# The order of two steps in the state-space scan: both halves of the x_dt transposes in one place, the product of the decay across chunks behind the segment sums

## The chip, the cores and the metric

The kernel runs on one core of one Trainium2 chip. The metric is the device time of one execution in microseconds (us). The changed kernel is timed against the one before; the time given is the median of several executions.

## The reference

One layer of a hybrid decoder: a Mamba-2 state-space branch (SSD) and a sparse attention branch work on the same normalised input of 256 tokens and 1024 channels, and are merged by gates. What matters here is the SSD branch, cut to its core:

```python
xdt = (xh * dt[..., None])                      # 32 heads of 64, 2 chunks of 128 tokens
a_cs = jnp.cumsum(adt, axis=2)                  # adt = dt * a
seg = a_cs[:, :, :, None] - a_cs[:, :, None, :]
decay = jnp.exp(jnp.where(causal, seg, -jnp.inf))
cb = jnp.einsum('bclgn,bcsgn->bclsg', c_, b_)
y_diag = jnp.einsum('bclsg,bclsgh,bcsghp->bclghp', cb, decay, xdt)
...
y_off = jnp.einsum('bclgn,bcghpn,bclgh->bclghp', c_, prev, jnp.exp(a_cs))
y = (y_diag + y_off) + xh * d_skip
y = rmsnorm_by_group(y * silu(z))               # 4 groups of 512 channels
```

The 32 heads form 4 groups of 8 heads. With only two chunks, the state that chunk 0 hands to chunk 1 needs no recurrence: its part of y is a product with a third decay matrix, "across" the two chunks.

## The kernel before

All weights come as 133 units of 128x1024 float32 (512 KB each) through seven buffers `w_raw`. Almost every unit (a split unit) is made into a high part `w_hi` by ACT (L924) and a low part `w_lo`, of which DVE subtracts the first six or seven eighths (L1185) and POOL the rest (L1527). PE then needs 24 matmuls of 256 columns for the unit (L696 to L698: high by high, low by high, high by low), into one of three banks `gemm0` to `gemm2`. ACT and DVE read the tile out.

What each engine does, and in what order, is one hand-written table, `schedule()`. `put(u, ...)` hangs steps behind unit u. PE and POOL work through it in the order STEPS: unit u, then its steps. ACT and DVE work through LATE_STEPS: the steps of unit u stand one unit later, behind what they do for unit u+1. No engine leaves its own order; semaphores alone join them.

Units 13 to 44 are the projections x and z: four x tiles and four z tiles for each group. The scan of group g is hung at b = 20 + 8g and what follows, so b is unit 20, 28, 36 and 44. The steps are, with q a half group of four heads (a quad, two for each group):

- xt (g, c): PE transposes the four x tiles of chunk c into a small bank (L743); DVE multiplies them by dt into `x_dt` (L1382) and sets the bank free.
- seg q: PE forms the segment sums of both chunks in the two score banks (L757, L758); ACT takes the exponential (L1082, `decay`); DVE multiplies chunk 0 by C·B (L1389, `cb_decay`), POOL chunk 1 (L1588).
- ea q: PE forms the sums across the chunks in a small bank (L764); ACT takes the exponential (L1088, `decay_across`); POOL multiplies by C·B (L1599, `cb_decay_across`) and then makes the rows `seg_moving` for the next quad (L1539, two instructions).
- y q: PE multiplies (L784 with `cb_decay`, L787 with `cb_decay_across`) into the bank `y_or_o`; DVE adds the skip (L1395) and multiplies by the z gate (L1400).
- ysq, ysum, ssq, yn: the norm of the group before. ACT squares (L1093), POOL adds up (L1593, L1594), PE sums over the partitions in a small bank (L794), ACT takes the root (L1098, with a table load before and after it), DVE takes the reciprocal (L1404) and normalises (L1409, L1413).

There are two small banks, used in turn by all steps that need one. Before a step writes its bank, PE waits until the step two before it has been read out:

```python
def begin_small(key):
    n = T_IDX[key]
    if n >= 2:
        pe.wait_ge(t_free[n % 2], n // 2)
    return TB[n % 2]
```

The order of use within a group is xt (g, 0), xt (g, 1), ea 2g, ssq g-1, ea 2g+1. So ea 2g waits for the DVE instruction L1382 of xt (g, 0), and ssq g-1 for that of xt (g, 1). The step ssq g-1 also waits for POOL's two sums; y q waits for L1389, L1588 and L1599 of its quad. Below, a scan step's number is that of its quad, 0 to 7.

Of the kernel before, what the change touches and what calls it, by code (L numbers as in the profile page):

```python
# [77 lines left out]
def schedule():  # L78

    after = {}

    def put(u, *steps):
        after.setdefault(u, []).extend(steps)

    put(len(PAIRS) - 2, ("ada2", 0))
    put(6, ("dtT", 0))
    put(7, ("dtA", 0), ("dtE", 0))
    put(8, ("dtB", 0), ("dtL", 0))
    put(10, ("dtC", 0))
    put(13, ("acs", 0))
    for kind in range(3):  # L100
        put(15 + kind, ("cb", kind))
    ssq_after = 12
    for g in range(SSM_GROUPS):
        b = 20 + 8 * g
        put(b, ("xt", (g, 0)))
        put(b + 1, ("xt", (g, 1)), ("seg", 2 * g))
        put(b + 2, ("ea", 2 * g))
        put(b + 4, ("y", 2 * g), ("seg", 2 * g + 1))
        put(b + 5, ("ea", 2 * g + 1))
        put(b + 7, ("y", 2 * g + 1))  # L110
        put(b + 8, ("ysq", g))
        put(b + 10, ("ysum", g))
        put(b + ssq_after, ("ssq", g))
        for j in range(TPG + 2):
            for ahead, name in ((2, "ynlo"), (1, "ynhi"), (0, "yn")):
                if 0 <= j - ahead < TPG:
                    put(b + ssq_after + 2 + j, (name, TPG * g + j - ahead))
    for g in range(KV_GROUPS):
        put(18 + 8 * g, ("blk0", g))
        put(19 + 8 * g, ("blk1", g))  # L120
    put(47, ("clear", 0))
    at = UNITS.index
    put(at(("w1k", 0, 3)) + 2, ("hidT", 0))
    put(at(("w1v", 0, 3)) + 2, ("hidT", 1))
    put(at(("w1v", 0, 3)) + 1, ("kcp", 0))
    put(at(("w1v", 0, 3)) + 4, ("vcp", 0))
    put(at(("vs", 1, 0)) + 2, ("vt", 0))
    put(at(("w1v", 0, 3)) + 3, ("zero", 0))
    tiles = [u for u, unit in enumerate(UNITS) if unit[0] != "ag"]
    q7 = tiles.index(at(("q", 7, 0)))  # L130

    def after_tile(n, *steps):
        put(tiles[n], *steps)

    after_tile(q7 + 1, ("cs", 0), ("cs", 1))
    after_tile(q7 + 2, ("cs2", 0))
    after_tile(q7 + 3, ("vt", 1))
    after_tile(q7 + 5, ("ct", 0), ("ct", 1))
    t0 = q7 - 2
    after_tile(t0 - 3, ("kpos", 0))  # L140
    for h in range(ATT_HEADS):
        after_tile(t0 - 2 + 2 * h, ("q2", h))
    for h in range(ATT_HEADS):
        after_tile(t0 + 2 * h, ("sc", h))
        after_tile(t0 + 1 + 2 * h, ("ex", h))
        after_tile(t0 + 2 + 2 * h, ("ps", h))
        after_tile(t0 + 4 + 2 * h, ("pt", h))
    last_h = tiles.index(at(("mg", 15, 0)))
    for p in range(ATT_HEADS // 2):
        after_tile(t0 + 8 + 4 * p + (p == 0), ("pv", p))  # L150
        after_tile(max(last_h + 3, t0 + 8 + 4 * p), ("osp", p))
    put(at(("nsa", 4, 0)), ("agB", 0))
    put(at(("nsa", 6, 0)), ("agB", 1))
    steps = []
    for u in range(len(UNITS)):
        steps.append(("gemm", u))
        steps += after.get(u, [])
    steps += [("flush", 0)]

    late = []  # L160
    for u in range(len(UNITS)):
        late += [("gemm", u)] + after.get(u - 1, [])
    late += [("flush", 0)] + after.get(len(UNITS) - 1, [])
    return steps, late


STEPS, LATE_STEPS = schedule()
SPLIT_IDX, NATIVE_IDX, TILE_IDX = {}, {}, {}
for _u, (_kind, _j, _part) in enumerate(UNITS):
# [1582 lines left out]
```

## Time and profile before

| | us |
|---|---|
| median of 3 runs | 475.51 |
| lowest and highest | 475.44, 476.58 |
| the profiled execution | 475.58 |
| its span in the trace | 473.8 |
| PE busy | 439.2 (93%) |
| DVE busy | 353.0 (75%) |
| ACT busy | 264.7 (56%) |
| POOL busy | 231.1 (49%) |

The profiled execution lies within 0.1 us of the median. The span is 1.8 us shorter than its time; what lies around it has no instructions. In the views below a matmul's duration runs from its start to its modelled end, so starts are read against starts. "Idle before" is time in which an engine had nothing running, with what released it.

### The profile page before, as it was taken

The numbers are of one execution on the slowest core, as the hardware profiler recorded it, in microseconds if no ns is written. First come the engines' busy times: TensorE is split into PE (matmuls) and PEld (weight loads), VectorE is DVE, ScalarE is ACT, GpSimd is POOL, SyncE is SP. The second block draws the span as 40 slices with busy tenths as digits, with TensorE's granted clock in tenths as the row PEclk, the third lists the DMA queues.
The fourth block names the chain that finished last, engine by engine and source line by source line (L and its number), as shares of the span: only waits on it lengthen the run. The fifth ranks groups of instructions, "written<-read, shape, count | busy, mean of one in ns | idle before, by whom it ended". The sixth has DMA issues, their size and how long they took to land.

```text
span 473.8 us, 9880 instructions
## 1 busy us (share of the span) xinstructions
PE 439.2 (93%) x3640; PEld 402.2 (85%) x3640; DVE 353.0 (75%) x617; ACT 264.7 (56%) x518; POOL 231.1 (49%) x236
## 2 busy tenths in 40 slices
PE   2689989999999996999889999999999999999995
PEld 2287989999999986987789999889898999999874
DVE  0375789999999999968684876768696766547733
ACT  3245785755566646644697844656566464534441
POOL 0154662368697557683365542244445362445340
PEclk9779999999999998999999998999999999999999
DMA  8998544564424532527609840625747433556102
GB/s 291 420 413 343 180 135 133 192 205 139 151 74 134 177 117 70 178 84 260 224 6 385 291 170 0 222 96 218 258 144 255 147 126 122 162 193 246 46 0 89
DMA packets 22391, 84.04 MB, mean 177 GB/s; under 512 B 2492, under 2 KB 2882, under 8 KB 21186
## 3 DMA queue, kind: packets, MB, share of 16 engines
q1 hardware_dynamic: 22344, 83.42, 49.7%
q8 instruction: 29, 0.48, 0.4%
q14 instruction: 18, 0.15, 0.1%
HBM read 82.36 MB, written 1.05 MB: 176 GB/s over the span
## 4 chain that ended last, share of the span: by engine, by line
PE 70%; DVE 9%; issue 7%; ACT 5%; POOL 4%; DMA 3%; SPq 1%; DVEq 0%; POOLq 0%; ACTq 0%
PE gemm L696 15%; PE gemm L698 15%; PE gemm L697 15%; DMA w_ada_shift_scale<-in_w_ada 3%; PE y_or_o L902 2%; DVE w_lo L1185 2%; ACT w_hi L924 2%; PE y_or_o L784 1%; DVE conv_acc L1232 1%; ACT probs L1143 1%; PE score L866 1%; POOL w_lo L1527 1%; PE small L577 1%; PE gemm L655 1%; PE score L868 1%
## 5 line engine op out<-in xcount | busy, mean ns | idle before, releaser
L1527 POOL TENSOR_TENSOR w_lo<-w_raw,w_hi 128x256 fp32r<-128x256 f32 (+1 forms) x117 | 132.2, 1135 | 175.6 <-ACT w_hi L924 140.9
L696 PE MATMUL gemm<-h_hi,w_hi 128*128 128x256 f32 x600 | 173.1, 289 | 2.7 <-DVE conv_acc L1232 2.0
L697 PE MATMUL gemm<-h_lo,w_hi 128*128 128x256 f32 x600 | 168.5, 281 | 0.0
L698 PE MATMUL gemm<-h_hi,w_lo 128*128 128x256 f32 x600 | 168.4, 281 | 0.0
L1185 DVE TENSOR_TENSOR w_lo<-w_raw,w_hi 128x768 fp32r<-128x768 f32 (+1 forms) x117 | 132.0, 1129 | 43.6 <-ACT w_hi L924 42.9
L924 ACT CAST w_hi<-w_raw 128x1024 fp32r<-128x1024 f32 x117 | 122.1, 1046 | 52.4 <-PE gemm L698 29.4
L696 PEld LDWEIGHTS gemm<-h_hi,w_hi 128*128 128x128 f32 x600 | 114.7, 191 | 5.4 <-issue 2.5
L697 PEld LDWEIGHTS gemm<-h_lo,w_hi 128*128 128x128 f32 x600 | 114.2, 190 | 0.5
L698 PEld LDWEIGHTS gemm<-h_hi,w_lo 128*128 128x128 f32 x600 | 114.5, 191 | 0.0
L696 PE MATMUL gemm<-ynorm_hi,w_hi 128*128 128x256 f32 x128 | 36.4, 284 | 0.0
L698 PE MATMUL gemm<-ynorm_hi,w_lo 128*128 128x256 f32 x128 | 35.6, 278 | 0.0
L697 PE MATMUL gemm<-ynorm_lo,w_hi 128*128 128x256 f32 x128 | 35.6, 278 | 0.0
L1232 DVE SCALAR_TENSOR_TENSOR conv_acc<-gemm,conv_half,conv_acc 128x255 f32<-128x255 f32 (+2 forms) x66 | 31.6, 479 | 2.8 <-ACT conv_acc L957 1.2
L1143 ACT ACTIVATE probs<-score,softmax_small 128x128 f32<-128x128 f32 (+1 forms) x64 | 26.0, 422 | 1.5 <-DVE softmax_small L1448 1.5
L957 ACT ACTIVATE conv_acc<-gemm,conv_half 128x256 f32<-128x256 f32 x22 | 12.4, 564 | 25.1 <-DVE x_conv_T L1194 15.4
L1588 POOL TENSOR_TENSOR cb_decay<-decay,cb_T 128x512 f32<-128x512 f32 x8 | 12.1, 1511 | 27.0 <-ACT decay L1082 19.3
L696 PEld LDWEIGHTS gemm<-ynorm_hi,w_hi 128*128 128x128 f32 x128 | 24.1, 188 | 0.7 <-issue 0.7
L1539 POOL TENSOR_TENSOR seg_moving<-acs_rows,consts 128x512 fp32r<-128x512 f32 x16 | 20.6, 1309 | 8.2 <-DVE acs_cols L1374 8.2
L698 PEld LDWEIGHTS gemm<-ynorm_hi,w_lo 128*128 128x128 f32 x128 | 24.2, 189 | 0.0
L697 PEld LDWEIGHTS gemm<-ynorm_lo,w_hi 128*128 128x128 f32 x128 | 24.0, 188 | 0.0
L1150 ACT COPY probs_T<-small 128x512 f32<-128x512 f32 x16 | 9.5, 593 | 19.8 <-PE y_or_o L902 19.8
L931 ACT ACTIVATE tanh_tmp<-gemm 128x256 f32<-128x256 f32 x24 | 9.2, 385 | 19.5 <-PE gemm L698 17.4
(253 smaller groups left out, 897.3 us busy)
## 6 DMA issues: line engine op xcount, KB each, us to landing
w_raw<-in_wpack SPq DMA_DIRECT2D x133, 512.0 KB, 4.3
w_ada_shift_scale<-in_w_ada SPq DMA_DIRECT2D x8, 1024.0 KB, 15.7
x_T<-in_xT SPq DMA_DIRECT2D x2, 512.0 KB, 5.9
x_residual<-in_x_tok SPq DMA_DIRECT2D x1, 1024.0 KB, 4.8
out_tok_dram<-out_tok SPq DMA_DIRECT2D x4, 256.0 KB, 2.1
ada_gate_products<-in_gate_bias SPq DMA_DIRECT2D x1, 512.0 KB, 4.8
g_post_rows<-in_g_post_rows SPq DMA_DIRECT2D x1, 512.0 KB, 5.7
consts<-in_consts SPq DMA_DIRECT2D x1, 272.0 KB, 22.7
```

Source lines behind the costliest of these rows:

```text
L696: nc.tensor.matmul(bank[:, 0:SEQ], w_hi, hi[:, k0 + k, :], start=first, stop=False)
L697: nc.tensor.matmul(bank[:, 0:SEQ], w_hi, lo[:, k0 + k, :], start=False, stop=False)
L698: last = nc.tensor.matmul(bank[:, 0:SEQ], w_lo, hi[:, k0 + k, :], start=False, stop=end)
L924: nc.scalar.copy(WH[:, n % HI_SLOTS, :], RAW[:, u % RAW_SLOTS, :]).then_inc(hi_ready, 1)
L957: nc.scalar.activation(ACC[:, ci % 2, :], bank, ACT.Identity, bias=CW[:, 96 + col:97 + col], scale=CW[:, 4 * col + 3:4 * col + 4]).then_in ...
L1143: last = nc.scalar.activation(E[:, k, b, P * qt:P * qt + nk], SB[qt][:, nk * b:nk * b + nk], ACT.Exp, bias=SM[:, k, 0, c:c + 1], accum_out ...
L1150: nc.scalar.copy(PT[:, i % 2, :, 0:SEQ], bank[:, :].rearrange("p (b q) -> p b q", b=2)).then_inc(release, 1)
L1185: nc.vector.tensor_tensor(WL[:, n % LO_SLOTS, 0:c], RAW[:, u % RAW_SLOTS, 0:c], WH[:, n % HI_SLOTS, 0:c], ALU.subtract).then_inc(lo_ready, 1)
L1232: ins = nc.vector.scalar_tensor_tensor(ACC[:, ci % 2, s:SEQ], bank[:, 0:SEQ - s], CW[:, 4 * col + tap:4 * col + tap + 1], ACC[:, ci % 2, s ...
L1527: nc.gpsimd.tensor_tensor(WL[:, n % LO_SLOTS, c:1024], RAW[:, u % RAW_SLOTS, c:1024], WH[:, n % HI_SLOTS, c:1024], ALU.subtract).then_inc( ...
L1539: nc.gpsimd.tensor_tensor(MV[:, c, :, :], TP[:, c, :].unsqueeze(1).to_broadcast([P, 4, P]), oh, ALU.mult).then_inc(mv_done, 1)
L1588: nc.gpsimd.tensor_tensor(MM[:, 1, :, :], EX[:, 1, :, :], CB[:, 1, i // 2, :].unsqueeze(1).to_broadcast([P, 4, P]), ALU.mult).then_inc(mm_ ...
```

## The change

In the part of `schedule()` for the scan, xt (g, 1) moves from unit b+1 to unit b, ea 2g from b+2 to b+1, and ea 2g+1 from b+5 to b+4. Since the table drives all engines, the transposes, DVE's products by dt, ACT's exponential, POOL's product and POOL's next rows all move with their step.

```diff
     for g in range(SSM_GROUPS):
         b = 20 + 8 * g
-        put(b, ("xt", (g, 0)))
-        put(b + 1, ("xt", (g, 1)), ("seg", 2 * g))
-        put(b + 2, ("ea", 2 * g))
-        put(b + 4, ("y", 2 * g), ("seg", 2 * g + 1))
-        put(b + 5, ("ea", 2 * g + 1))
+        put(b, ("xt", (g, 0)), ("xt", (g, 1)))
+        put(b + 1, ("seg", 2 * g), ("ea", 2 * g))
+        put(b + 4, ("y", 2 * g), ("seg", 2 * g + 1), ("ea", 2 * g + 1))
         put(b + 7, ("y", 2 * g + 1))
         put(b + 8, ("ysq", g))
         put(b + 10, ("ysum", g))
```

No instruction is added or removed, and the order in which the small banks are used stays as it was. The changed file has two lines less, so in its rows every line number from there on is smaller by 2.

On PE at seg 6 (group 3, unit b+1 = 45), before:

```order
L698 MATMUL gemm2<-h_hi_52,w_lo_56 128x256
L743 MATMUL small0<-consts_60,x_conv_T_89 128x128 x4
L757 MATMUL score0<-seg_moving_95,acs_cols_72 128x512
L758 MATMUL score0<-mask_sl_bf16_62,ident_bf16_61 128x512
L757 MATMUL score1<-seg_moving_95,acs_cols_72 128x512
L758 MATMUL score1<-mask_sl_bf16_62,ident_bf16_61 128x512
L696 MATMUL gemm0<-h_hi_52,w_hi_55 128x256
```

and in the change:

```order
L696 MATMUL gemm2<-h_hi_52,w_lo_56 128x256
L755 MATMUL score0<-seg_moving_95,acs_cols_72 128x512
L756 MATMUL score0<-mask_sl_bf16_62,ident_bf16_61 128x512
L755 MATMUL score1<-seg_moving_95,acs_cols_72 128x512
L756 MATMUL score1<-mask_sl_bf16_62,ident_bf16_61 128x512
L762 MATMUL small1<-seg_moving_95,acs_cols_72 128x512
L694 MATMUL gemm0<-h_hi_52,w_hi_55 128x256
```

The transposes of chunk 1 into `small0` have gone ahead of unit 45, and ea 6 into `small1` stands ahead of unit 46, where it used to stand behind it.

On DVE at the same place, where `x_dt` is made, before:

```order
L1194 SCALAR_TENSOR_TENSOR z_gate_then_y_75<-tanh_tmp_108,gemm1 128x256
L1185 TENSOR_TENSOR w_lo_56<-w_raw_54,w_hi_55 128x768
L1413 TENSOR_TENSOR ynorm_lo_77<-y_tmp_101,ynorm_hi_76 128x256
L1409 SCALAR_TENSOR_TENSOR y_tmp_101<-z_gate_then_y_75,params_59,rstd_y_102 128x256
L1382 TENSOR_TENSOR x_dt_92<-small1,dt_68 128x512
L1194 SCALAR_TENSOR_TENSOR z_att_then_o_78<-tanh_tmp_108,gemm2 128x256
```

and in the change:

```order
L1192 SCALAR_TENSOR_TENSOR z_gate_then_y_75<-tanh_tmp_108,gemm1 128x256
L1183 TENSOR_TENSOR w_lo_56<-w_raw_54,w_hi_55 128x768
L1411 TENSOR_TENSOR ynorm_lo_77<-y_tmp_101,ynorm_hi_76 128x256
L1407 SCALAR_TENSOR_TENSOR y_tmp_101<-z_gate_then_y_75,params_59,rstd_y_102 128x256
L1380 TENSOR_TENSOR x_dt_92<-small1,dt_68 128x512
L1380 TENSOR_TENSOR x_dt_92<-small0,dt_68 128x512
L1192 SCALAR_TENSOR_TENSOR z_att_then_o_78<-tanh_tmp_108,gemm2 128x256
```

The instruction that frees `small1` for ea 6 keeps its place in DVE's order; the one that frees `small0` follows it at once.

On POOL around quad 6, before:

```order
L1588 TENSOR_TENSOR cb_decay_97<-decay_96,cb_T_93 128x512
L1527 TENSOR_TENSOR w_lo_56<-w_raw_54,w_hi_55 128x256
L1593 TENSOR_TENSOR y_sq_100<-y_sq_100 128x512
L1594 TENSOR_TENSOR y_sq_100<-y_sq_100 128x256
L1599 TENSOR_TENSOR cb_decay_across_99<-decay_across_98,cb_T_93 128x512
L1539 TENSOR_TENSOR seg_moving_95<-acs_rows_71,consts_60 128x512 x2
```

and in the change:

```order
L1586 TENSOR_TENSOR cb_decay_97<-decay_96,cb_T_93 128x512
L1597 TENSOR_TENSOR cb_decay_across_99<-decay_across_98,cb_T_93 128x512
L1537 TENSOR_TENSOR seg_moving_95<-acs_rows_71,consts_60 128x512 x2
L1525 TENSOR_TENSOR w_lo_56<-w_raw_54,w_hi_55 128x256
L1591 TENSOR_TENSOR y_sq_100<-y_sq_100 128x512
L1592 TENSOR_TENSOR y_sq_100<-y_sq_100 128x256
```

The across product and the next rows come first now, and the two sums for the norm of the group before stand behind them. Quads 2 and 4 have the same pattern.

## Rows read from the trace of the kernel before

**Rows 1.** Waits of PE alone, 100 to 215 us: us, times, longest.
```profile
PE y_or_o L784 <- POOL cb_decay_across L1599: 5.7, 3, 4.2
```

**Rows 2.** Timeline of PE, y 5 and after: start, us, [idle before <-releaser].
```profile
180.38 0.28 PE L698 MATMUL gemm<-h_hi,w_lo 128*128 128x256 f32 x1
184.82 0.66 PE L784 MATMUL y_or_o<-cb_decay,x_dt 128*64 128x128 f32 x8 [4.16 <-POOL cb_decay_across L1599]
...
186.63 0.58 PE L696 MATMUL gemm<-h_hi,w_hi 128*128 128x256 f32 x1
...
190.70 0.60 PE L743 MATMUL small<-consts,x_conv_T 128*128 128x128 f32 x4
191.05 0.37 PE L696 MATMUL gemm<-h_hi,w_hi 128*128 128x256 f32 x1
```

**Rows 3.** Windows: length; busy PE, PEld, DVE, ACT, POOL; PEclk, DMA share, GB/s.
```profile
107.00:181.00 74.00, 72.13 (x639) 67.54 (x637) 72.67 (x107) 44.88 (x73) 50.52 (x50) 1.00 0.39 129
...
186.00:189.00 3.00, 3.00 (x18) 2.67 (x16) 2.93 (x4) 0.41 (x1) 2.92 (x5) 0.50 0.03 5
```

**Rows 4.** Timeline of PE, from seg 6 to the end of seg 7.
```profile
194.23 0.48 PE L757 MATMUL score<-seg_moving,acs_cols 128*128 128x512 f32 x1
...
195.06 0.47 PE L696 MATMUL gemm<-h_hi,w_hi 128*128 128x256 f32 x1
...
197.98 0.39 PE L764 MATMUL small<-seg_moving,acs_cols 128*128 128x512 f32 x1
...
203.87 0.59 PE L794 MATMUL small<-y_sq,consts 128*128 128x256 f32 x2
...
206.05 0.49 PE L757 MATMUL score<-seg_moving,acs_cols 128*128 128x512 f32 x1
...
207.19 0.47 PE L696 MATMUL gemm<-h_hi,w_hi 128*128 128x256 f32 x1
```

**Rows 5.** Timeline of DVE: first dt products of groups 2 and 3, and between.
```profile
160.66 0.69 DVE L1382 TENSOR_TENSOR x_dt<-small,dt 128x512 f32<-128x512 f32 x1
...
181.10 1.14 DVE L1194 SCALAR_TENSOR_TENSOR x_conv_T<-tanh_tmp,conv_acc 128x256 f32<-128x256 f32 x1 [0.27 <-ACT tanh_tmp L966]
...
195.87 0.69 DVE L1382 TENSOR_TENSOR x_dt<-small,dt 128x512 f32<-128x512 f32 x1
```

**Rows 6.** Timeline of ACT, quad 5.
```profile
179.51 1.09 ACT L1082 ACTIVATE decay<-score 128x512 f32<-128x512 f32 x2
180.48 0.42 ACT L966 ACTIVATE tanh_tmp<-conv_acc 128x256 f32<-128x256 f32 x1
...
181.98 0.62 ACT L1088 ACTIVATE decay_across<-small 128x512 f32<-128x512 f32 x1
```

**Rows 7.** Timeline of ACT, a tile read out behind y 7.
```profile
213.46 0.38 ACT L931 ACTIVATE tanh_tmp<-gemm 128x256 f32<-128x256 f32 x1 [2.18 <-PE gemm L698]
```

**Rows 8.** Timeline of POOL, quad 5.
```profile
180.67 1.28 POOL L1588 TENSOR_TENSOR cb_decay<-decay,cb_T 128x512 f32<-128x512 f32 x1 [7.61 <-PE gemm L698]
...
182.68 1.88 POOL L1599 TENSOR_TENSOR cb_decay_across<-decay_across,cb_T 128x512 f32<-128x512 f32 x1
```

**Rows 9.** Timeline of PE, the unit behind seg 4.
```profile
158.78 0.47 PE L696 MATMUL gemm<-h_hi,w_hi 128*128 128x256 f32 x1
```

**Rows 10.** Timeline of POOL, quad 6.
```profile
197.57 1.33 POOL L1588 TENSOR_TENSOR cb_decay<-decay,cb_T 128x512 f32<-128x512 f32 x1 [4.22 <-ACT decay L1082]
...
199.74 1.48 POOL L1593 TENSOR_TENSOR y_sq<-y_sq 128x512 f32<-128x512 f32 x1
...
202.33 2.00 POOL L1599 TENSOR_TENSOR cb_decay_across<-decay_across,cb_T 128x512 f32<-128x512 f32 x1
204.29 2.40 POOL L1539 TENSOR_TENSOR seg_moving<-acs_rows,consts 128x512 fp32r<-128x512 f32 x2
```

**Rows 11.** Timeline of DVE, one w_lo while POOL is idle.
```profile
174.42 1.09 DVE L1185 TENSOR_TENSOR w_lo<-w_raw,w_hi 128x896 fp32r<-128x896 f32 x1
```

**Rows 12.** DVE by line and form, 107 to 196 us: busy us, mean ns.
```profile
L1185 DVE TENSOR_TENSOR w_lo<-w_raw,w_hi 128x896 fp32r<-128x896 f32 x18 | 26.9, 1495 | 0.0
```

## The prediction

> **What bounds the kernel now.** I read first the list of PE's waits over the stretch that the change touches. PE works nearly without a gap there and waits for one thing only: three times for `cb_decay_across` ahead of a y step, 5.7 us in all, of which 4.2 in one wait [rows 1]. That one is in front of y 5: the matmul before it starts at 180.38, y 5 at 184.82 [rows 2]. It costs more than its own length. From 186 to 189 the granted clock is 0.50, the lower level of 1.2 GHz [rows 3], and unit 44 takes 190.70 - 186.63 = 4.07 us [rows 2], where three units and one ea product take 203.87 - 195.06 = 8.81 us at full clock, at most 2.94 each [rows 4]. The low clock thus costs some 1.1 us on this unit and a little on y 5; I take 1.3.
>
> Then I looked for what stands behind that wait. In the windows view DVE is busy 72.67 of the 74 us from 107 to 181 [rows 3]; its list of instructions shows no stop from 107 to 181.10, where it waits 0.27 us for ACT, and none from there to the dt product at 195.87 [rows 5]. So two engines are full here. PE is ahead, DVE behind by several us, and ACT waits for DVE. The exponentials of quad 5 come at 179.51 for that reason [rows 6]; PE made their sums well before. Every semaphore by which PE waits for a late DVE instruction is therefore dangerous: PE is fast only because nothing ties it closely to DVE. Behind y 7 it is PE that leads: ACT waits 2.18 us for a gemm before it reads a tile [rows 7], so a delay that PE has by then is carried to the end.
>
> **What the change takes away.** Nothing is added; only places move.
>
> y 5. POOL's product of chunk 1 ends at 180.67 + 1.28 = 181.95; the across product starts at 182.68, because ACT made its exponential only at 181.98, behind two tanh and a cast, and ends at 184.56 [rows 6, 8]. Now the exponential stands directly behind the `decay` ones, which end at 180.60, and is done by 181.2. The across product starts at 181.95 and, at its 1.88 us, ends at 183.8. y 5 starts at 184.1 instead of 184.82: 0.7 us gained, not the 4.2 of the wait, since what is late next is the `decay` exponential itself, which hangs on DVE. The other two waits, 5.7 - 4.2 = 1.5 us in sum, go as well, but PE then only waits longer in front of y 5, so they are worth nothing.
>
> The rows for seg 7. Seg 7 takes 207.19 - 206.05 = 1.14 us against 195.06 - 194.23 = 0.83 for seg 6 [rows 4], as its second sum waits for `seg_moving`, finished at 204.29 + 2.40 = 206.69 [rows 10]. POOL now makes these rows earlier: 0.3 us gained, and about 0.2 more because y 6 no longer comes right behind the across product that ends at 204.33. Together 0.5.
>
> **What it adds: ea 2g waits for DVE.** The ea product of an even quad writes the small bank that xt (g, 0) used, and DVE's dt product frees it. Before, one unit of matmuls (2.9 us) lay between seg and ea and covered this. Now ea stands directly behind seg. In group 2 PE is through with seg 4 at 158.78 [rows 9], and DVE's product runs from 160.66 to 161.35 [rows 5]: a new wait of 2.6 us. That wait, like the smaller one of group 1, costs nothing in the end, because PE has the long wait before y 5 to lose it in.
>
> Group 3 has no such reserve. PE arrives so: y 5 starts at 184.1, takes 1.81 (186.63 - 184.82), unit 44 takes 2.9, the two transposes 0.35 each (191.05 - 190.70), unit 45 2.8 and seg 6 0.83, which makes 193.2 in all [rows 2, 4]. The dt product runs from 195.87 to 196.56 [rows 5]. DVE's work up to it is the same list, but its gate at 181.10 waited for a tanh (180.48) that now stands behind the across exponential of 0.62 [rows 5, 6]; that shifts DVE by about 0.5 us. The bank is free at 197.06, and ea 6 starts at 197.2. PE has idled 4.0 us there. Before, unit 46 started at 195.06 and ssq 2 at 203.87 with unit 46, ea 6 and two more units in 8.81 us [rows 4]. The same work now starts at 197.2 and ends at 206.0, which is 2.1 us later.
>
> The clock. A stop of 4.16 us before y 5 was followed by the low clock [rows 2, 3]. The new stop of 4.0 us is nearest to that row, so I take that the clock falls again, for 1.3 us: ssq 2 at 207.3. The old fall goes, with its stop cut into two short waits, but its gain lies ahead of the wait for DVE and is swallowed by it like the rest.
>
> **Also added: the sums of the norm stand behind POOL's run.** From 197.57 on POOL now does the product of chunk 1 (1.33), the across product (2.00), the next rows (2.40), one `w_lo` (0.84, from 198.90 to 199.74) and then the two sums (202.33 - 199.74 = 2.59): they end at 206.7 instead of 202.33 [rows 10]. ssq 2 needs them. At 207.3 they are hidden by PE's own delay, but if the clock does not fall they are last and hold ssq 2 until 206.8. In groups 1 and 2 the same shift makes PE wait 1 to 2 us at ssq 0 and ssq 1; it is lost in the wait before y 5.
>
> **The moved work itself.** POOL's `w_lo` of unit b+5 comes some 4 to 5 us later, but PE reads it only in the last part of that unit, over 8 us on; the same holds for the weight load that waits for it, seven units ahead. If both covers were gone it would be a unit's wait, 2.9 us; I count nothing. The second dt product on DVE comes one unit earlier (0.69 us) and delays that unit's `w_lo` by as much, with three units of lead; nothing. Fewer changes between gemm and small products could give PE a gain below what I can read; between -0.5 and +0.5, taken as nothing.
>
> **The sum.** ssq 2 starts at 207.3 instead of 203.87, +3.4; less 0.5 for y 6 and seg 7 gives +2.9 us. After that PE leads and the rest of the program follows it. Against the profiled execution of 475.58 (span 473.8) that is 478.5; the median before lies 0.07 lower, so 478.4.
>
> **A cost that no row settles: DVE and POOL slow each other.** A `w_lo` of 896 columns takes 1.09 us on DVE while POOL is idle [rows 11], but 1.495 in the mean of 18 between 107 and 196 us [rows 12]: 18 x 0.4 = 7.3 us of DVE's time is lost there beside POOL, on this line alone. The change packs POOL's instructions differently against DVE's. The forecast holds only if that loss stays. A quarter of it more or less moves the dt product of group 3 by 1.8 us, and PE with it. I take no shift, for POOL does the same work, and keep these ends.
>
> The Trainium skill (SBUF — State Buffer, Who interferes with whom) says that a DVE instruction with two inputs in SBUF contends with a GpSimd instruction that reads SBUF, the later one being blocked whole, and that one with a single SBUF input does not. The trace agrees with its first half [rows 11, 12]. By it the loss depends on which of the two starts first, so a packed run of POOL can give DVE time back as well as take it; it is the reason for the second rival below, and the sum does without it.
>
> **Rivals.**
> 1. The clock does not fall at ea 6. For it: the stop is a little shorter than 4.16 us. Then ssq 2 starts at 206.0 by PE and 206.8 by POOL's sums: +2.9 - 0.5 = +2.4 at most, +1.6 if the sums come in time. 477.5.
> 2. Faster: DVE reaches the dt product of group 3 early, because the packed POOL run collides less with it. It needs half of the 7.3 us, 3.7: the bank is free at 193.4, when PE comes, and ea 6 does not wait. Then the 0.7 of y 5, the 1.3 of the old low clock and the 0.5 behind it all remain: 475.5 - 2.5 = 473.0. It turns from loss to gain once DVE is about 2.5 us earlier, since the clock holds then too. Against it: POOL's work is not less.
> 3. The waits cancel: DVE gains 1 to 2 us, or the clock stays and the sums are early. 475.5, within 1.4.
> 4. DVE loses 1.8 us more, or PE falls to the low clock a second time at ea 4 and comes late to everything: 480.3.
>
> That the change does not do what it says is excluded by the order of instructions.
>
> **How the numbers follow.** Chances: forecast 0.42, rival 1 0.18, rival 2 0.13, rival 3 0.19, rival 4 0.08. A difference of 0.3% is 1.4 us, about what a measurement here can tell from none. The forecast and rival 4 are slower in full (0.50) and of rival 1 two thirds (0.12): slower 0.62. Rival 2 with a little of rival 3 is faster, 0.16; the rest, 0.22, is within. The range leaves out the ends of rivals 2 and 4: 474.3 to 480.6.
>
> **What would show it.** Right: among PE's waits after the change the y steps nearly vanish, and `small` L762 <- DVE `x_dt` L1380 appears, longest at group 3 with 3.5 to 4.5 us, then about 2.5 at group 2; low granted clock behind seg 6 instead of behind y 5; a wait of 1 to 2 us of L792 for POOL's `y_sq` in groups 1 and 2. Wrong: no wait of ea 6, or the dt product of group 3 well before 196 us, which would mean that DVE's time was not fixed; or a delay at unit 51 that is no longer there at the end, which would mean that another engine led behind y 7.

## The result and the profile after

| us | before | after |
|---|---|---|
| median | 475.48 (474.75 to 476.58, 4 runs) | 481.39 (479.91 to 481.85, 4 runs) |
| profiled execution | 475.58 | 479.91 |
| its span | 473.8 | 478.1 |
| PE, DVE, ACT, POOL busy | 439.2, 353.0, 264.7, 231.1 | 439.8, 353.1, 264.8, 233.4 |

The change makes the kernel slower: ratio 1.0103, 95% interval 1.0080 to 1.0125. That is +5.9 us in the median and +4.3 us between the two profiled executions. The ratio is a figure over all runs and not the quotient of the two medians, which is 1.0124; by the ratio the loss is 4.9 us. The same holds for the ratios below. The profiled execution of after is the fastest of its four. The trace shown below therefore explains 4.3 us, and what the others have on top is taken up with the first experiment.

PE's waits alone, 100 to 215 us (us, times, longest), where before had only [rows 1]:

```profile
PE small L762 <- DVE x_dt L1380: 5.3, 2, 4.0
PE small L792 <- POOL y_sq L1592: 4.6, 3, 2.6
PE y_or_o L782 <- POOL cb_decay_across L1597: 0.7, 1, 0.7
```

The 5.7 us of before are down to 0.7, and 9.9 us have come in their place. PE's timeline (start, us, [idle before <-releaser]), from ssq 0 to ssq 2:

```profile
140.69 0.67 PE L792 MATMUL small<-y_sq,consts 128*128 128x256 f32 x2 [2.62 <-POOL y_sq L1592]
...
162.77 0.50 PE L762 MATMUL small<-seg_moving,acs_cols 128*128 128x512 f32 x1 [1.30 <-DVE x_dt L1380]
...
172.66 0.67 PE L792 MATMUL small<-y_sq,consts 128*128 128x256 f32 x2 [1.21 <-POOL y_sq L1592]
...
184.99 0.66 PE L782 MATMUL y_or_o<-cb_decay,x_dt 128*64 128x128 f32 x8 [0.67 <-POOL cb_decay_across L1597]
...
192.99 0.39 PE L755 MATMUL score<-seg_moving,acs_cols 128*128 128x512 f32 x1
...
198.04 0.80 PE L762 MATMUL small<-seg_moving,acs_cols 128*128 128x512 f32 x1 [3.98 <-DVE x_dt L1380]
...
208.84 0.67 PE L792 MATMUL small<-y_sq,consts 128*128 128x256 f32 x2 [0.78 <-POOL y_sq L1592]
```

Seg 6 comes 1.24 us earlier than in [rows 4] (192.99 against 194.23), and ea 6 then waits 3.98 us for a bank that DVE has not read out. In the windows view (length; busy PE, PEld, DVE, ACT, POOL; PEclk, DMA share, GB/s) the low clock has moved from behind y 5 [rows 3] to behind ea 6:

```profile
186.00:189.00 3.00, 3.00 (x32) 2.83 (x29) 2.96 (x3) 0.35 (x1) 3.00 (x4) 1.00 0.02 5
198.00:200.00 2.00, 1.96 (x8) 1.86 (x9) 2.00 (x4) 1.47 (x3) 1.00 (x1) 0.50 0.63 229
107.00:181.00 74.00, 68.88 (x615) 63.96 (x614) 71.65 (x108) 44.43 (x71) 49.84 (x48) 1.00 0.39 136
```

From 107 to 181 us PE is busy 68.88 us instead of 72.13, and DVE still 71.65 of 74 [rows 3]. DVE is nearly full as before, but no longer without a stop. Its timeline at the places of [rows 5], and the one stop that before has no row for:

```profile
147.57 1.48 DVE L1192 SCALAR_TENSOR_TENSOR x_conv_T<-tanh_tmp,conv_acc 128x256 f32<-128x256 f32 x1 [1.21 <-ACT tanh_tmp L964]
...
182.91 0.67 DVE L1192 SCALAR_TENSOR_TENSOR x_conv_T<-tanh_tmp,conv_acc 128x256 f32<-128x256 f32 x1 [0.76 <-ACT tanh_tmp L964]
...
197.30 1.28 DVE L1380 TENSOR_TENSOR x_dt<-small,dt 128x512 f32<-128x512 f32 x2
```

POOL at quad 6, against [rows 10]:

```profile
199.00 1.92 POOL L1586 TENSOR_TENSOR cb_decay<-decay,cb_T 128x512 f32<-128x512 f32 x1 [4.21 <-ACT decay L1080]
200.88 1.47 POOL L1597 TENSOR_TENSOR cb_decay_across<-decay_across,cb_T 128x512 f32<-128x512 f32 x1
202.31 2.67 POOL L1537 TENSOR_TENSOR seg_moving<-acs_rows,consts 128x512 fp32r<-128x512 f32 x2
...
206.35 1.47 POOL L1591 TENSOR_TENSOR y_sq<-y_sq 128x512 f32<-128x512 f32 x1
207.90 0.79 POOL L1592 TENSOR_TENSOR y_sq<-y_sq 128x256 f32<-128x256 f32 x1
```

The sums end at 208.69, and ssq 2 at 208.84 had waited for them.

To compare traces I count from y 0 on PE, since what lies ahead of it varies by about 1 us between executions whose order there is the same (y 0 starts at 108.93 in before, at 109.36 in after). This leaves out what the new order does in group 0 ahead of y 0. From y 0 to y 7 before takes 214.26 - 108.93 = 105.33 us and after 218.82 - 109.36 = 109.46. So 4.1 of the 4.3 us arise in this stretch.

### The profile page after: what moved, and what is told of

The parts are those of the page before. It is cut to its first block, busy times and chain, and to the rows that moved or that the text cites. A ratio compares the mean times of both kernels' runs of the same rounds, so it can differ in the third digit from the quotient of the medians.

```text
span 478.1 us, 9880 instructions
## 1 busy us (share of the span) xinstructions
PE 439.8 (92%) x3640; PEld 402.6 (84%) x3640; DVE 353.1 (74%) x617; ACT 264.8 (55%) x518; POOL 233.4 (49%) x236
## 4 chain that ended last, share of the span: by engine, by line
PE 60%; issue 11%; POOL 11%; DVE 9%; ACT 5%; DMA 3%; SPq 1%; DVEq 0%; POOLq 0%; ACTq 0%
PE gemm L694 12%; PE gemm L696 12%; PE gemm L695 12%; DMA w_ada_shift_scale<-in_w_ada 3%; POOL seg_moving L1537 3%; POOL w_lo L1525 3%; PE y_or_o L900 2%; DVE w_lo L1183 2%; POOL cb_decay_across L1597 2%; ACT w_hi L922 2%; POOL cmp_blocks L499 2%; ACT probs L1141 1%; DVE conv_acc L1230 1%; PE score L864 1%; PE gemm L653 1%
## 5 line engine op out<-in xcount | busy, mean ns | idle before, releaser
L1525 POOL TENSOR_TENSOR w_lo<-w_raw,w_hi 128x256 fp32r<-128x256 f32 (+1 forms) x117 | 134.6, 1156 | 176.6 <-ACT w_hi L922 141.9
L694 PE MATMUL gemm<-h_hi,w_hi 128*128 128x256 f32 x600 | 171.1, 285 | 2.7 <-DVE conv_acc L1230 2.0
L1183 DVE TENSOR_TENSOR w_lo<-w_raw,w_hi 128x768 fp32r<-128x768 f32 (+1 forms) x117 | 129.9, 1110 | 43.7 <-ACT w_hi L922 42.9
L1586 POOL TENSOR_TENSOR cb_decay<-decay,cb_T 128x512 f32<-128x512 f32 x8 | 13.1, 1634 | 32.3 <-ACT decay L1080 32.3
L1537 POOL TENSOR_TENSOR seg_moving<-acs_rows,consts 128x512 fp32r<-128x512 f32 x16 | 21.6, 1369 | 8.2 <-DVE acs_cols L1372 8.2
```

What stands on the lines that cost most here:

```text
L694: nc.tensor.matmul(bank[:, 0:SEQ], w_hi, hi[:, k0 + k, :], start=first, stop=False)
L1183: nc.vector.tensor_tensor(WL[:, n % LO_SLOTS, 0:c], RAW[:, u % RAW_SLOTS, 0:c], WH[:, n % HI_SLOTS, 0:c], ALU.subtract).then_inc(lo_ready, 1)
L1525: nc.gpsimd.tensor_tensor(WL[:, n % LO_SLOTS, c:1024], RAW[:, u % RAW_SLOTS, c:1024], WH[:, n % HI_SLOTS, c:1024], ALU.subtract).then_inc( ...
L1537: nc.gpsimd.tensor_tensor(MV[:, c, :, :], TP[:, c, :].unsqueeze(1).to_broadcast([P, 4, P]), oh, ALU.mult).then_inc(mv_done, 1)
L1586: nc.gpsimd.tensor_tensor(MM[:, 1, :, :], EX[:, 1, :, :], CB[:, 1, i // 2, :].unsqueeze(1).to_broadcast([P, 4, P]), ALU.mult).then_inc(mm_ ...
```

## The experiments

All kernels compute the whole output. Each edit is shown against before, unless it says otherwise, with b = 20 + 8g. The runs were made in four groups, and each group has its own runs of before. Their medians were 476.37 (18 runs; the change again and the parts one at a time), 476.67 (22; ea 6 late, the sums earlier, the transposes earlier), 476.46 (17; the transposes again, the late y steps) and 476.32 (16; the last kernel). The result above has 475.48. So a median is best set against the before of its own group. My theory was that the cost is the wait of ea 6 for DVE, with the clock that falls behind it, and POOL's later sums as a second part. The rivals were a loss of DVE's own time, and a cost in moving the transposes.

### The change again

> The changed order once more, for a second trace and more times. Its profiled execution took 479.9 us, other executions up to 481.9. Theory (PE waits at ea 6 for DVE's dt product, and then runs at the low clock): 480 to 482 us; in the trace ea 6 again starts within 0.5 us behind the end of the dt product of group 3, and the additional time of a slower execution is found in a longer low clock or in a later dt product. Rival (the extra loss lies somewhere behind y 7): the two traces agree up to unit 51 and differ behind it.

Measured: 481.98 (481.27 to 482.32, 4 runs), ratio 1.0128 (1.0106 to 1.0150). Its profiled execution, 482.32, is one of the long ones, and differs from that of after (479.91) in group 1. PE's timeline and the windows view of this kernel:

```profile
140.96 0.67 PE L792 MATMUL small<-y_sq,consts 128*128 128x256 f32 x2 [2.61 <-POOL y_sq L1592]
```

```profile
142.00:145.00 3.00, 3.00 (x23) 2.21 (x19) 2.93 (x7) 2.95 (x4) 0.49 (x2) 0.51 0.61 224
```

The stop before ssq 0 is the same as in after (2.61 and 2.62 us), but here the granted clock falls to 0.51 behind it, where after has 1.00 from 142 to 145. Seg 3 starts at 143.89 instead of 142.75, which is 0.9 us later behind y 0. What follows is seen on ACT and DVE, in this kernel:

```profile
145.23 1.22 ACT L1080 ACTIVATE decay<-score 128x512 f32<-128x512 f32 x2
146.34 0.59 ACT L1086 ACTIVATE decay_across<-small 128x512 f32<-128x512 f32 x1
148.90 0.42 ACT L964 ACTIVATE tanh_tmp<-conv_acc 128x256 f32<-128x256 f32 x1 [1.97 <-PE gemm L696]
```

```profile
149.52 0.82 DVE L1192 SCALAR_TENSOR_TENSOR x_conv_T<-tanh_tmp,conv_acc 128x256 f32<-128x256 f32 x1 [2.89 <-ACT tanh_tmp L964]
```

and in after, on ACT:

```profile
145.94 0.60 ACT L1086 ACTIVATE decay_across<-small 128x512 f32<-128x512 f32 x1
146.95 0.42 ACT L964 ACTIVATE tanh_tmp<-conv_acc 128x256 f32<-128x256 f32 x1 [0.41 <-PE gemm L696]
```

Before, that tanh started at 145.18, straight behind the `decay` exponentials, and DVE had no stop there. Now the across exponential (0.60 us) stands ahead of it, and the gemm tile that it reads comes late, by 0.41 us in after and by 1.97 in this execution. DVE, which has no time to spare, stops for 1.21 and 2.89 us. The waits of DVE alone, from 107 us to its dt product of group 3, are 0.5 us in before, 2.0 in after and 4.1 here. From y 0 to y 7 this execution takes 110.83 us, 1.4 more than after. So of the 2.4 us between these two executions 1.4 arise here, from the same stop of PE with a different clock behind it; 0.3 lie ahead of y 0 and 0.8 behind y 7. One long and one short execution have a trace; that the others are long for the same reason is not shown.

### One part at a time

The transposes alone, run twice:

```diff
-        put(b, ("xt", (g, 0)))
-        put(b + 1, ("xt", (g, 1)), ("seg", 2 * g))
+        put(b, ("xt", (g, 0)), ("xt", (g, 1)))
+        put(b + 1, ("seg", 2 * g))
```

> Only the transposes of chunk 1 go up to unit b; the ea products stay where they were before. Theory (the loss is ea 2g waiting for DVE, and POOL's sums behind the across product): neither is there, so 475.5 us, within 1 us, with the same 4 us wait before y 5. Rival (putting both halves in one place loads DVE and delays its chain): a third or more of the loss, 477.5 us or above, with DVE's dt product of group 3 later than 196.5 us.

> The transposes alone moved, once more, for a second trace and more times (the first gave a ratio of 1.006, its trace only 0.7 us more between the first y and the last). Theory (moving the transposes costs little by itself): ratio 1.000 to 1.003 over more executions, and the trace again has less than 1 us between y 0 and y 7 more than before the change. Rival (both dt products in one place hold up DVE's chain): ratio 1.004 to 1.008, and the decay exponential of quad 5 comes at least 1.5 us later behind y 0 than before (70.6 us).

The ea of the even quads alone (ea 2g still stands behind seg 2g, but xt (g, 1) keeps its place):

```diff
-        put(b + 1, ("xt", (g, 1)), ("seg", 2 * g))
-        put(b + 2, ("ea", 2 * g))
+        put(b + 1, ("xt", (g, 1)), ("seg", 2 * g), ("ea", 2 * g))
```

> Only the even ea products (0, 2, 4, 6) go directly behind their segment sums; the transposes and the odd ea products stay. Theory: this part alone carries the loss: ea 6 waits about 4 us for the dt product, ssq 0 to 2 wait for POOL's sums, and the time is 480 to 482 us. The second transposes still stand where the bank of ssq is concerned as before. Rival (the loss needs both halves of the change together): 477 us or below.

The ea of the odd quads alone:

```diff
-        put(b + 4, ("y", 2 * g), ("seg", 2 * g + 1))
-        put(b + 5, ("ea", 2 * g + 1))
+        put(b + 4, ("y", 2 * g), ("seg", 2 * g + 1), ("ea", 2 * g + 1))
```

> Only the odd ea products (1, 3, 5, 7) go directly behind their segment sums. Theory: this is the part that gains: y 5 starts 0.7 us earlier, since POOL's across product follows its product of chunk 1 at once, and nothing waits for DVE; 474.8 us, or 473.3 if the shorter stop before y 5 (3.5 us) no longer brings the low clock. Rival (the across exponential in front of tanh delays DVE as much as it helps POOL): 475.5 to 476.5 us.

| kernel | median | ratio, 95% interval | y 0 to y 7, against before |
|---|---|---|---|
| transposes | 478.07 (7 runs) | 1.0060 (1.0036 to 1.0084) | +0.7 |
| transposes again | 478.00 (12) | 1.0038 (1.0021 to 1.0055) | +1.4 |
| even ea | 478.95 (6) | 1.0059 (1.0032 to 1.0086) | +2.9 |
| odd ea | 476.15 (10) | 0.9994 (0.9977 to 1.0012) | -0.2 |

The last column comes from one trace each. The three parts add up to 0.9 to 1.1%, nearly the 1.03 and 1.28% of the whole change. PE's waits from 100 to 215 us of the odd ea:

```profile
PE y_or_o L783 <- POOL cb_decay_across L1598: 4.6, 3, 3.2
```

and of the even ea:

```profile
PE small L763 <- DVE x_dt L1381: 4.0, 2, 2.6
PE small L793 <- POOL y_sq L1593: 2.5, 2, 1.6
PE y_or_o L783 <- POOL cb_decay_across L1598: 1.5, 1, 1.5
```

The odd ea takes 1.1 us off PE's waits (5.7 to 4.6) and the time stays the same within its interval, where a gain had been expected. In its trace the gain at y 5 is there and is then lost. Behind y 0, y 5 comes at 74.43 us instead of 75.89, but y 6 at 95.42 instead of 95.66. Over the 5 us from y 5 on the granted clock is 0.50 in the mean, where before has 0.66, and y 6 has a new wait of 0.26 us. DVE's stops for a tanh grow from 0.3 to 1.1 us, as the rival said. So a shorter wait brought nothing here; that each of those waits is worth nothing is not shown.

The even ea brings both new waits and about half of the loss, less than the whole loss that was expected of it. Its stop of 2.63 us before ea 6 was followed by the low clock (0.72 in the mean from 196 to 202).

The transposes alone should have cost nothing by my theory. In the medians they cost 1.7 and 1.5 us in two separate measurements, and by the ratios 2.9 and 1.8. The second one lies between what theory and rival had said. Their waits of PE are those of before, a little longer in one:

```profile
PE y_or_o L784 <- POOL cb_decay_across L1599: 5.6, 3, 4.2
```

```profile
PE y_or_o L784 <- POOL cb_decay_across L1599: 7.2, 4, 4.2
```

(the first run, then the second). Both traces have 0.5 us more from y 5 to y 7. In the first the low clock lasts longer there (0.52 in the mean over the 5 us from y 5 on, against 0.66 in before); in the second y 6 has a new wait of 0.80 us for the across product. The rest of the +0.7 and +1.4 lies ahead of y 5: quad 5's exponentials come 0.2 and 0.9 us later behind y 0, and in the second run those of quad 3 are already 1.3 us later. DVE stops for 0.3 and 0.5 us only, so it is not a stop on DVE that costs here. Why the exponentials come later I could not pin to one row, and these are single traces; the cause of what the transposes cost stays open. A part may lie in group 0 ahead of y 0: the six traces with both transposes at unit b have y 0 at 109.36 to 110.15 us, the four that keep them apart, with y in its place, at 108.48 to 109.83, and these ranges overlap.

### What the wait of ea 6 is worth

The change, with ea 6 alone put back behind unit 46:

```diff
-        put(b + 1, ("seg", 2 * g), ("ea", 2 * g))
+        put(b + 1, ("seg", 2 * g))
+        put(b + 1 + (g == 3), ("ea", 2 * g))
```

(this diff is against the change).

> The changed order, but ea 6 alone goes back to unit 46, where it stood before. Theory (the stop in front of ea 6 and the low clock behind it carry most of the loss, the stops of groups 1 and 2 nothing): 4.0 us of stop and 1.3 of clock go, the across product of quad 6 then waits for its exponential as before; 476.5 to 478 us, 3.5 to 5 us below the changed kernel. Rival (DVE's later work carries the loss, the stop at ea 6 only shows it): 480 us or above, with another wait of PE of 3 us or more behind seg 6.

Measured: 479.18 (477.48 to 480.11, 9 runs), ratio 1.0048 (1.0031 to 1.0065). That is 2.5 us above its own before, where the change is 5.9 and 5.6 above its own; so 3.1 to 3.4 us less (2.2 and 2.8 between the medians themselves). It is about half of the loss and below the 3.5 to 5 us that I had expected. Its waits of PE from 184 to 215 us tell why it is not more:

```profile
PE y_or_o L783 <- ACT rstd_y L1097: 1.4, 1, 1.4
PE small L763 <- DVE x_dt L1381: 1.2, 1, 1.2
PE y_or_o L783 <- POOL cb_decay_across L1598: 0.7, 1, 0.7
PE small L793 <- POOL y_sq L1593: 0.5, 1, 0.5
```

Even one unit later ea 6 still waits 1.2 us. The next two stops follow from POOL's list at quad 6, which starts 1.4 us later behind y 0 than in before (199.73 us). The sums hold ssq 2 for 0.5 us. The stop of 1.4 us at y 6 is put down to `rstd_y`, which y does not wait for in the code; the across product that it does wait for stands behind the sums and ends at 207.05, and y 6 starts at 207.30. Behind these stops the clock falls after all (0.60 from 208 to 212). DVE's dt product of group 3 comes 88.38 us behind y 0 in this kernel, 1.4 later than in before (86.94). That delay arises before group 3, and moving ea 6 does not touch it. So the wait of ea 6 is worth about half of the loss; the other half has other sources.

### What POOL's late sums are worth

The change, with the sums one unit earlier, so that on POOL they stand ahead of the next group's first products again:

```diff
-        put(b + 10, ("ysum", g))
+        put(b + 9, ("ysum", g))
```

(this diff is against the change).

> The changed order, and in addition POOL's two sums for the norm go from unit b+2 to b+1, in front of the product of chunk 1, where POOL was idle for 4 us. Theory: the waits of ssq 0 to 2 for POOL (4.6 us in all) disappear, but only the one of ssq 2 (0.8 us) lies behind the last stop for DVE, so 0.5 to 1 us below the changed kernel, 480.5 to 481 us. Rival (the waits in groups 1 and 2 do pass on, because PE's delay holds up DVE): 3 us or more below, 478.5 us or less.

Measured: 480.49 (479.05 to 481.22, 4 runs), ratio 1.0070 (1.0046 to 1.0095), PE's waits from 100 to 215 us:

```profile
PE small L762 <- DVE x_dt L1380: 8.8, 2, 4.7
```

The wait for `y_sq` is gone from all groups, 4.6 us, and the time falls by less: 0.9 and 1.5 us against the two medians of the change, 1.8 to 2.1 us when each is set against its own before. That lies between theory and rival, so the waits of groups 1 and 2 pass on in part. PE comes earlier to ea 4 and ea 6 and waits longer there, 4.69 and 4.11 us, with the low clock behind both (0.58 from 164 to 168, 0.51 from 198 to 202). Most of the stop has only changed its place. Nor is DVE free: it stops for 0.37 and 0.76 us at quad 3, nearly the 1.21 of after, though PE no longer stops before ssq 0. Its dt product of group 3 comes 88.31 us behind y 0, later than in after (87.94).

### The transposes a unit earlier

If DVE's dt product came earlier, ea 2g would find its bank free. The change, with both transposes at unit b-1:

```diff
-        put(b, ("xt", (g, 0)), ("xt", (g, 1)))
+        put(b - 1, ("xt", (g, 0)), ("xt", (g, 1)))
```

(this diff is against the change), alone and together with the sums at b+9:

> The changed order, but both halves of the transposes stand at unit b-1, directly behind y of the group before; DVE's two dt products move with them by one unit. Theory (ea 2g waits only because DVE reaches the dt product late): DVE makes it 3 to 4 us earlier, ea 4 and ea 6 wait less than 1 us, the clock stays high behind seg 6; the sums on POOL then hold ssq 2 by 1 to 2 us; 476 to 477.5 us. Rival (having both products in one place costs as such): 478 us or above, though the waits at ea have gone.

> The transposes at unit b-1 and POOL's sums at unit b+1, with the ea products behind the segment sums. Theory: no wait at ea, none at ssq; what stays is PE's stop before y 5, which hangs on DVE's chain. y 5 starts 0.7 us earlier than before the change, and if its stop is short or missing the low clock of 1.3 us goes too: 473 to 475 us, below both kernels. Rival (the total of DVE's work up to y 5, with POOL beside it, grows by the new order): 476 us or above.

Alone it is the slowest of the kernels made from the change: 484.91 (484.42 to 485.21, 4 runs), ratio 1.0172 (1.0153 to 1.0191), where I had expected 476 to 477.5. With the sums earlier it is 478.29 (476.99 to 479.73, 12 runs), ratio 1.0040 (1.0024 to 1.0055), where I had expected 473 to 475. Both miss, and both are in the range of the rival. DVE's dt product of group 3 was to come 3 to 4 us earlier; behind y 0 it comes at 87.55 and 86.59 us, 0.4 and 1.4 earlier than in after. PE's waits from 100 to 215 us, alone:

```profile
PE small L792 <- POOL y_sq L1592: 10.0, 3, 4.2
PE small L762 <- DVE x_dt L1380: 2.0, 1, 2.0
PE y_or_o L782 <- POOL cb_decay_across L1597: 0.4, 1, 0.4
```

and together:

```profile
PE y_or_o L782 <- POOL cb_decay_across L1597: 3.1, 1, 3.1
PE small L762 <- DVE x_dt L1380: 2.2, 2, 2.0
PE y_or_o L782 <- DVE cb_decay L1387: 1.6, 1, 1.6
```

Alone, the wait for DVE shrinks as meant, from 5.3 to 2.0 us, but PE runs on into POOL's sums (10.0 us), the clock falls twice (0.72 from 140 to 146, 0.50 from 212 to 216), and DVE has the stop of the long executions again: 3.6 us for `tanh_tmp`. With late sums, a PE that comes earlier loses more at ssq than it gained, and DVE stops with it. The kernel with both edits has no longer wait than 3.1 us, but the low clock stands behind that one (0.72 in the mean from 184 to 190), and it is still not faster than before.

### Is PE's wait before y 5 worth anything?

Before's order, with every y one unit later, so that PE has gemms to do while POOL works. The second kernel also has the odd ea and the sums earlier:

```diff
-        put(b + 4, ("y", 2 * g), ("seg", 2 * g + 1))
-        put(b + 5, ("ea", 2 * g + 1))
-        put(b + 7, ("y", 2 * g + 1))
+        put(b + 4, ("seg", 2 * g + 1))
+        put(b + 5, ("y", 2 * g), ("ea", 2 * g + 1))
+        put(b + 8, ("y", 2 * g + 1))
```

> The order from before the change, with every y step one unit later (b+5 and b+8); nothing else moves but that seg 2g+1 now stands ahead of y 2g. Theory (PE stops for what DVE, ACT and POOL deliver late, and a unit of matmuls put in front of the waiting step fills the stop): the 5.7 us of waits before y 3, 4 and 5 shrink to at most 1.5, the low clock behind y 5 is gone (1.3), but group 3 then runs into DVE's chain sooner: 470 to 474 us. Rival (PE's lead over DVE is all taken back at the next step, as in the changed kernel): 475 us or above, with a new wait of 2 us or more at ea 6 or y 6.

> As the late y steps, and in addition the odd ea products directly behind their segment sums and POOL's sums for the norm at unit b+1. Theory: the across products of quads 3, 5 and 6 come 0.7 to 2 us earlier and no stop is left before ssq or y; 469 to 473 us, below the late y steps alone by 0.5 to 2 us. Rival (the across product was not last any more, so nothing is gained): the same as the late y steps alone within 0.5 us.

Measured: 487.04 (485.11 to 488.09, 4 runs), ratio 1.0215 (1.0174 to 1.0257), and 484.37 (482.61 to 487.60, 4 runs), ratio 1.0176 (1.0133 to 1.0218). I had expected 470 to 474 of the first and 469 to 473 of the second; they are the largest misses of the study. The wait before y 5 is gone, as meant, but PE has new waits and DVE stops too. The waits of PE and of DVE from 100 to 215 us, and the windows row, in the first kernel:

```profile
PE score L757 <- POOL seg_moving L1539: 6.8, 5, 2.1
PE small L794 <- POOL y_sq L1594: 4.0, 2, 2.5
DVE cb_decay L1389 <- issue: 4.3, 2, 2.4
DVE conv_acc L1232 <- ACT conv_acc L957: 2.9, 4, 1.0
DVE cb_decay L1389 <- ACT decay L1082: 1.5, 1, 1.5
```

```profile
107.00:181.00 74.00, 67.64 (x553) 61.47 (x553) 66.67 (x99) 39.62 (x66) 51.00 (x49) 0.94 0.33 122
```

DVE is busy 66.67 of the 74 us instead of 72.67 [rows 3]. Two things come together. The first is on DVE: there is one `cb_decay` buffer, and in the code the products of quad q, on DVE and on POOL, wait until y of quad q-1 has read it. At quad 1 the exponentials are ready at 112.1, PE's last matmul of y 0 starts at 114.82, and DVE's product at 115.68, after a stop of 1.89 us. At quad 3 the stop is 2.44 us, but only the last 0.9 of it are the buffer's (exponentials ready at 147.3, product at 148.24); the rest is a late exponential. The second is on PE: seg 2g+1 now stands ahead of y 2g and waits for POOL's rows, 6.8 us in five waits, and ssq 4.0 more. PE's waits are 11.1 us in sum instead of 5.7, and the stop of 2.05 us before seg 3 was followed by the low clock (0.50 from 141 to 144). How the loss divides between the two is not shown. The second kernel has the same two (6.4 us for `seg_moving`, DVE's stops at `cb_decay`). So a later y is not free: it keeps a buffer longer that DVE and POOL need.

### The best of the parts together

Before, with the odd ea behind its seg and the sums at b+9:

> The order from before the change with two edits that make nobody wait for DVE: the odd ea products directly behind their segment sums, and POOL's two sums for the norm at unit b+1. Theory (DVE's chain up to the dt product of group 3 is the bound, PE's stops only show it): the waits before y 3 and y 4 (1.5 us) go, the stop before y 5 stays and grows by as much, the low clock behind it stays; y 6 comes up to 1 us earlier; 474.5 to 476.5 us, ratio 0.997 to 1.001. Rival (PE's stops are losses of their own): 1.5 us and more are gained, ratio 0.996 or below.

Measured: 475.74 (474.00 to 478.59, 12 runs), ratio 0.9989 (0.9966 to 1.0011). PE's waits go from y 5 to ea 4 and ea 6 in part:

```profile
PE y_or_o L783 <- POOL cb_decay_across L1598: 3.3, 2, 2.9
PE small L763 <- DVE x_dt L1381: 2.8, 2, 2.0
```

The time is as expected, but not for the reason given: the stop before y 5 was to grow and the low clock to stay. No stop is over 2.9 us and the clock stays at 1.00 from 184 to 190, yet nothing is gained that can be measured. No kernel of this study is faster than before.

## Why the prediction was right, and where not

The direction and the mechanism hold: a new wait of ea 6 for DVE, a low clock behind it, and POOL's later sums. The size is too small: +2.9 us were forecast, +4.3 came in the profiled execution and +5.9 in the median, which at 481.39 lies 0.8 us above the range. By the ratio the loss is 4.9 us and the time 480.4, just inside it. Step by step, in the profiled execution:

**PE waits only for the across product, and the wait is worth little.** Right as far as it was tested. The odd ea takes 1.1 us of it and the time stays; what y 5 gains is lost by y 6. Both attempts to move the wait elsewhere gained nothing.

**y 5 starts 0.7 us earlier.** The local gain is there and larger: from quad 5's first exponential to y 5 it is 184.99 - 180.83 = 4.16 us instead of 184.82 - 179.51 = 5.31 [rows 2, 6]. It did not help, since the exponential itself was 0.9 us later behind y 0. The low clock behind y 5 went, as said.

**DVE's shift: 0.5 us forecast, 1.0 measured, and by other means.** Counted from y 0, the dt product of group 3 comes at 87.94 instead of 86.94 us. The stop at 182.91 is 0.76 us instead of 0.27 [rows 5], the 0.5 of the forecast. What I had not seen is the stop of 1.21 us at quad 3, on the same pattern one group earlier. Together DVE stops 1.7 us more; 0.7 of it came back, since its instructions took less time.

**The new wait of ea 6.** Forecast 4.0 us, measured 3.98. The work of unit 46 starts 86.13 us behind y 0 in before (195.06 - 108.93, [rows 4]), and ea 6, now ahead of it, 88.68 in after: +2.55 us, where the forecast has +2.1. The wait itself says little, since seg 6 comes earlier; what counts is when DVE frees the bank.

**The clock.** From ea 6 to ssq 2 it takes 208.84 - 198.04 = 10.80 us instead of 8.81 [rows 4], 1.99 more. Less the 0.78 us of the stop before ssq 2 that is 1.2 us, forecast 1.3.

**POOL's sums were said to be hidden.** They were not: forecast end 206.7, real 208.69, so ssq 2 waited 0.78 us for them. The 2.0 us between are POOL's later start at quad 6, which hangs on DVE (199.00 against 197.57 in [rows 10], 1.4), and longer instructions: the product 1.92 instead of 1.33, and the `w_lo` ahead of the sums 1.45 instead of 0.84; the across product gave 0.5 back.

**The sum.** +2.55 for ea 6, +0.78 for the sums, +1.2 for the clock, less 0.4 at y 6 and seg 7 (forecast 0.5), is +4.1 us, as measured from y 0 to y 7. With 0.4 us from ahead of y 0 and 0.2 less behind y 7 it gives the +4.3; the delay was carried to the end, as forecast.

**The steps that failed.** The first is the sentence on the waits of groups 1 and 2, "costs nothing in the end, because PE has the long wait before y 5 to lose it in". PE can lose a delay there, but ACT and DVE can't. PE's stop before ssq 0 makes seg 3 and the gemm tile behind it late, ACT's tanh waits for that tile, and DVE for the tanh. I had priced the stop on PE alone. The waits of ea 4 and ssq 1 were 1.30 and 1.21 us, less than the 2.6 and within the 1 to 2 forecast, but that of ssq 0 was 2.62. The second is DVE's shift of 0.5 us: I took it at quad 5 only, and the across exponential stands ahead of the tanh at quad 3 as well. In after DVE stopped there for 1.21 us, of which 0.60 is that exponential and 0.41 the late tile; in the longer execution, where the clock also fell behind PE's stop, 2.89. So in the short execution the larger part is the exponential's, and only in the long one PE's stop. The kernel with early sums fits this: without a stop before ssq 0 DVE still stops 1.13 us at quad 3. The long trace also gives one way in which the median comes to lie above the profiled execution. How much of the +5.9 us the stop before ssq 0 carries, no run gives by itself. The third is that POOL's sums are hidden, at 0.78 us.

**The contention between DVE and POOL.** I kept it fixed and it moved, but the parts cancelled. DVE by line and form from y 0 to the dt product of group 3 (busy us, mean ns | idle before), before:

```profile
L1389 DVE TENSOR_TENSOR cb_decay<-decay,cb_T 128x512 f32<-128x512 f32 x5 | 3.9, 784 | 0.0
```

and after:

```profile
L1183 DVE TENSOR_TENSOR w_lo<-w_raw,w_hi 128x896 fp32r<-128x896 f32 x18 | 23.5, 1305 | 0.0
...
L1387 DVE TENSOR_TENSOR cb_decay<-decay,cb_T 128x512 f32<-128x512 f32 x5 | 6.5, 1291 | 0.0
```

The `w_lo` of 896 columns fall from 1495 ns [rows 12] to 1305, 3.4 us less in 18. The product on DVE rises from 784 to 1291 ns, 2.6 us more in five: at quads 1, 2 and 4 it takes 1.77, 1.78 and 1.52 us, while POOL makes its across product or its next rows, and at quads 3 and 5, where it starts about 0.5 us before POOL's product, 0.68 and 0.69. Over the whole stretch DVE's busy time is 0.7 us shorter (84.60 instead of 85.31). So the mechanism of the faster rival exists, but it is worth a fifth of the 3.7 us that it would have needed. The Trainium skill (SBUF — State Buffer, Who interferes with whom) says that a DVE instruction with two inputs in SBUF and one of GpSimd that reads SBUF exclude each other, and that the order of issue decides which of them waits. The two rows of after fit that: the loss moved from one line to another with POOL's order.

**The rivals.** That the clock doesn't fall, that the parts cancel and that DVE comes early are all refuted by the rows above. The rival "PE falls to the low clock a second time and comes late to everything", 480.3 us and 0.08, is close to what the one long trace shows, with the place in group 1 and not at ea 4. It deserved more. That DVE bounds the stretch up to y 6 is read from its list of instructions and fits all the runs; no run took work off DVE, which would be the direct test.

## What to carry to other kernels

Where PE is nearly full and waits for one thing only, look first for another engine whose list has no stop at all: here that is DVE, and by my reading PE's waits are the slack by which the two keep step. Before moving a step, follow each stop that it makes on PE to the next tile that the full engine needs, through the engine in between; a delay that PE can lose later may already have stopped the other. Do the same in each group that has the pattern, and not only in the last one. In these runs a wait that was removed by reordering mostly reappeared at the next semaphore that ties the two engines, so price that one before counting a gain.

## What the runs showed of the hardware

The granted clock is not a function of the stop alone. The same stop before ssq 0 of the changed kernel was followed by a clock of 0.51 from 142 to 145 us in one execution (2.61 us) and of 1.00 in another (2.62 us). The kernel with early transposes has both in one trace: 0.72 in the mean from 140 to 146 behind 2.64 us, and this row behind a stop of 3.09 us that ends at 173.35:

```profile
173.00:180.00 7.00, 6.65 (x60) 5.69 (x61) 6.86 (x13) 4.88 (x8) 1.94 (x3) 1.00 0.55 182
```

All stops of 3.98 us and more on PE in these traces, from y 0 to y 7, were followed by the low clock; of those between 2.6 and 3.2 us some were and some weren't. Shorter ones could be followed by it too: the late y steps have 0.50 from 141 to 144 behind a stop of 2.05 us. The Trainium skill (TensorE: Matmul & The Clock Gate, Part 1: The HAM clock gate) says of a kernel's start that the number of matmuls at the low clock differs from run to run of the same kernel. The two executions of the changed kernel show such a difference in mid-kernel: they are 0.9 us apart behind y 0 at seg 3, and 1.4 us at y 7.
